# Decoder trunk on one core: the scores of gated linear attention on 32-column strips, the norm's sum of squares in two rounded matmuls

## The chip, the cores and the metric

One core of a Trainium2 chip. The metric is the device time of one execution in microseconds; the kernel before has a median of 2439.63 us over 3 runs (2439.05 to 2439.84). Engines are called as in the profile: PE is TensorE's matmul, PEld its weight load, DVE is VectorE, ACT ScalarE, POOL GpSimd, SP the engine that queues transfers.

## The reference, cut to what matters

Two layers, one even (retention and a gated recurrence), one odd (gated linear attention, GLA), each with a squared-ReLU MLP, for a prompt of 1024 tokens and eight samples of 8 tokens (64 tokens). Only the odd layer's mixer is touched:

```
def step(s, blk):                       # one chunk of one head, C = 64 or 8 in the reference
    qc, kc, vc, gc = blk
    b = jnp.cumsum(gc, axis=1)
    diff = b[:, :, None] - b[:, None, :]
    w = jnp.exp(jnp.where(causal[None, :, :, None, None], diff, -jnp.inf))
    scores = jnp.einsum('bihd,bjhd,bijhd->bhij', qc, kc, w)
    o = (jnp.einsum('bhij,bjhe->bihe', scores, vc)
         + jnp.einsum('bihd,bhde->bihe', qc * jnp.exp(b), s))
    ...
o = head_rms(o) * norm_w                # x * rsqrt(mean(x*x) + eps) over the 256 values of a head
mix = (jax.nn.silu(r) * o.reshape(B, T, GLA_VALUE)) @ w_out
```

## The kernel before

Everything is kept transposed: 128 features on the partitions, 1088 tokens (1024 + 64) along the free side, in three groups of 384, 384 and 320 tokens (`GROUPS`). A float32 product of the large projections is made of three matmuls on rounded parts (high x high, high x low, low x high, `mm`, line 732); GpSimd and ScalarE split the weights, VectorE empties PSUM.

In the odd layer a list written out in Python (`odd_schedule`, from line 232) sets one order for all engines: each engine walks it and does its share of each item, in that order, so no engine overtakes its own list. Four heads of nine chunks (`ORDER`: prompt chunks 0 to 5, then the 64 sample tokens, then 6 and 7). Projections of later units fill the gaps: an `S` item is one unit and group, cut into two halves where it stands between score items.

The scores of a chunk of 128 tokens are not made with one decay per pair. For seven levels v (0 to 6) the chunk is cut into blocks of 2 x 2^v tokens; keys in the left half and queries in the right half of a block are scaled relative to the block's middle (items `X`, `XE`, `Q`, made by VectorE and ScalarE per group of three chunks, signalled by `lev_ready`), and a product of the two gives the scores that cross that middle. The diagonal itself comes from plain k and q. TensorE does this in `score` (from line 1137) in two parts:

- item `A` (from line 1194): three transposes (lines 1211, 1213), then the plain product k x q over the full 128 x 128 (line 1220), then the coarse levels 6, 5, 4, where only the wanted blocks are computed: one 64 x 64, two 32 x 32, four 16 x 16 matmuls (line 1153);
- then one half projection of the list;
- item `A2`: the fine levels 3 to 0. Each is one matmul with all 128 key columns as weights and the 64 right-half query columns moving (line 1159); of its result only the entries in the level's blocks are used. The last matmul raises `gsc_done`.

VectorE then waits for `gsc_done` and copies with masks (lines 2495, 2499) into the score matrix for item `B`. The chunk of 64 sample tokens has the plain product of 64 x 64 in `A` and three fine levels in `A2`. The score matmuls are in float32, not rounded; each such matmul leaves two records in the trace.

```
 1153  last = nc.tensor.matmul(flat[left:left + width, right], both[:, left:left + width], both[:, right], ...)
 1159  last = nc.tensor.matmul(out, keys, halves(both, v)[1], start=True, stop=True)
```

Norm of a head: `GN1` squares on ScalarE and adds the two halves on VectorE (line 2541); `GNM` sums over partitions with a matmul of ones in float32 (line 1300), takes the logarithm on ScalarE; `GN2` scales. There are 11 such sums; the twelfth is made apart.

## Time and profile before

| | |
|---|---|
| median of 3 runs | 2439.63 us |
| the profiled execution | 2441.21 us |
| its span, first to last instruction | 2439.1 us |
| PE / DVE / ACT / POOL busy | 99 / 54 / 33 / 50 % |
| mean granted TensorE clock | 0.993 |
| the odd layer's mixer | about 1180 to 1600 us of the span |

A row of the timeline gives the start, the time from the first start to the last end, engine, line, operation and tiles; for a matmul, 128*64 is the size of the weights (partitions x columns) and 128x64 what moves through. Records of PE overlap: the next matmul starts long before the one ahead of it has left the array. So costs are taken from start to start.

### The profile page before, as it was taken

How to read it: one execution, taken by the hardware profiler on the slowest of the kernel's cores; microseconds unless marked ns; L12 is line 12 of the kernel's file. 1: busy time of each engine (PE TensorE's matmuls, PEld its weight loads, DVE VectorE, ACT ScalarE, POOL GpSimd, SP SyncE). 2: the span in 40 equal slices, each digit the busy share in tenths (PEclk: the TensorE clock that was granted, in tenths of full speed). 3: DMA queues.
4: the chain of work that ended last, by engine and by line, in shares of the span. 5: the costliest groups of instructions: out<-in, count | busy, mean ns of one | idle time of the engine just before them, and what ended most of it. 6: DMA issues, size and time to landing. Idle time of an engine off the chain costs nothing. (4 is left out here: it accounts for less than half of the span.)

```text
span 2439.1 us, 42031 instructions
## 1 busy us (share of the span) xinstructions
PE 2423.2 (99%) x16160; PEld 2380.3 (98%) x16160; DVE 1305.2 (54%) x2047; ACT 796.2 (33%) x1254; POOL 1211.9 (50%) x1445
## 2 busy tenths in 40 slices
PE   9999999999999999999999999999999999999998
PEld 9999999999999999999999999999999999999998
DVE  6763354345545545566666665554345545445566
ACT  4711442222222223223444564442222222222234
POOL 2454136465675666675201111146565665666681
PEclk9999999999999999999999999999999999999999
DMA  4123031111111111113111111131111111111112
GB/s 151 35 63 89 26 119 44 53 44 44 52 44 44 52 53 41 47 53 117 47 42 63 47 50 58 34 128 44 44 44 53 53 44 44 53 45 43 53 53 83
DMA packets 41023, 140.04 MB, mean 57 GB/s; under 512 B 6320, under 2 KB 10032, under 8 KB 39696
## 3 DMA queue, kind: packets, MB, share of 16 engines
q1 hardware_dynamic: 32768, 106.78, 13.8%
q10 hardware_dynamic: 8080, 30.78, 3.5%
q8 instruction: 128, 2.10, 0.4%
q14 instruction: 47, 0.39, 0.0%
HBM read 120.42 MB, written 14.88 MB: 55 GB/s over the span
## 5 line engine op out<-in xcount | busy, mean ns | idle before, releaser
L732 PE MATMUL PS<-RB,WH 128*128 128x384 f32 (+1 forms) x4368 | 1087.7, 330 | 0.0
L732 PEld LDWEIGHTS PS<-RB,WH 128*128 128x128 f32 x4368 | 773.5, 189 | 7.5 <-issue 3.6
L732 PE MATMUL PS<-RA,WH 128*128 128x272 f32 (+2 forms) x3520 | 769.0, 309 | 1.3 <-DVE RA L1868 0.7
L732 PE MATMUL PS<-RB,WL 128*128 128x384 f32 (+1 forms) x2232 | 731.6, 328 | 0.0
L638 POOL TENSOR_TENSOR WH<-WR,FEW 128x256 fp32r<-128x256 f32 x420 | 320.1, 792 | 622.3 <-PE PS L732 593.0
L732 PEld LDWEIGHTS PS<-RA,WH 128*128 128x128 f32 x3520 | 586.9, 188 | 5.8 <-DVE RA L1868 1.0
L732 PE MATMUL PS<-RA,WL 128*128 128x272 f32 (+2 forms) x1760 | 540.6, 307 | 0.0
L732 PEld LDWEIGHTS PS<-RB,WL 128*128 128x128 f32 x2232 | 421.4, 189 | 0.0
L642 POOL TENSOR_TENSOR WL<-WR,WH 128x256 fp32r<-128x256 f32 x420 | 372.8, 917 | 0.0
L732 PEld LDWEIGHTS PS<-RA,WL 128*128 128x128 f32 x1760 | 330.7, 188 | 0.0
L1967 DVE TENSOR_TENSOR X<-PS,X 128x544 f32<-128x544 f32 x280 | 202.6, 724 | 205.2 <-PE PS L732 205.1
L1908 DVE SCALAR_TENSOR_TENSOR RAW<-PS,RS 128x384 f32<-128x384 f32 (+1 forms) x192 | 97.0, 533 | 351.1 <-PE PS L732 317.9
L732 PE MATMUL PS<-RA,WS 128*128 128x272 f32 x2016 | 272.1, 288 | 0.0
L732 PEld LDWEIGHTS PS<-RA,WS 128*128 128x128 f32 x2016 | 260.5, 188 | 0.0
L661 POOL TENSOR_TENSOR WL<-WR,WH 128x512 fp32r<-128x512 f32 x168 | 155.2, 938 | 183.4 <-ACT WH L1400 183.4
L650 POOL TENSOR_TENSOR WL<-WR,WH 128x256 fp32r<-128x256 f32 x88 | 67.0, 792 | 336.5 <-ACT WH L1698 336.5
L1381 ACT ACTIVATE RAW<-RAW 128x384 f32<-128x384 f32 (+1 forms) x192 | 92.2, 505 | 332.2 <-DVE RAW L1908 332.2
L1919 DVE TENSOR_TENSOR RA<-RAW,RA 128x544 fp32r<-128x544 f32 (+1 forms) x112 | 142.9, 1294 | 26.3 <-ACT RA L1389 17.4
L661 POOL TENSOR_TENSOR WS<-WR,WS 128x256 fp32r<-128x256 f32 x112 | 119.1, 1064 | 14.6 <-ACT WS L1413 14.6
L1967 DVE TENSOR_TENSOR GA<-PS,GA 128x544 f32<-128x544 f32 x112 | 81.2, 725 | 80.0 <-PE PS L732 79.3
L1892 DVE TENSOR_TENSOR X<-PS,EB 128x384 f32<-128x384 f32 (+1 forms) x48 | 25.4, 535 | 116.6 <-PE PS L732 116.6
L1348 ACT ACTIVATE RB<-X,FEW 128x1088 fp32r<-128x1088 f32 x24 | 28.7, 1205 | 161.9 <-DVE X L1892 125.7
(237 smaller groups left out, 2370.8 us busy)
## 6 DMA issues: line engine op xcount, KB each, us to landing
WR<-ws SPq DMA_DIRECT2D x189, 512.0 KB, 3.5
EB<-xT ACTq DMA_DIRECT2D x8, 544.0 KB, 5.9
x_spill<-X ACTq DMA_DIRECT2D x8, 544.0 KB, 3.1
EB<-x_spill ACTq DMA_DIRECT2D x8, 544.0 KB, 6.8
GA<-st_gla ACTq DMA_DIRECT2D x4, 1024.0 KB, 4.8
glas_o<-GA ACTq DMA_DIRECT2D x4, 1024.0 KB, 4.6
yT<-X SPq DMA_DIRECT2D x16, 208.0 KB, 1.9
X<-xT ACTq DMA_DIRECT2D x4, 544.0 KB, 6.0
```

The lines of the kernel that those rows point to most:

```text
L638: nc.gpsimd.tensor_tensor(WH[:, slot, QC * q:QC * (q + 1)], WR[:, slot, QC * q:QC * (q + 1)], ZERO[:, 0:1].to_broadcast([P, QC]), ALU.add) ...
L642: nc.gpsimd.tensor_tensor(WL[:, slot, QC * q:QC * (q + 1)], WR[:, slot, QC * q:QC * (q + 1)], WH[:, slot, QC * q:QC * (q + 1)].bitcast(F32 ...
L650: nc.gpsimd.tensor_tensor(WL[:, slot, QC * q:QC * (q + 1)], WR[:, slot, QC * q:QC * (q + 1)], WH[:, slot, QC * q:QC * (q + 1)].bitcast(F32 ...
L661: return nc.gpsimd.tensor_tensor(out, of, high.bitcast(F32), ALU.subtract)
L732: return nc.tensor.matmul(out, lhsT, rhs, start=start, stop=stop, skip_group_check=True)
L1348: A(dst[:, 0, k, :], X[:, k, :], ACT.Copy, scale=scale).then_inc(h_high, counts)
L1381: A(RAW[:, j, grp(g)], RAW[:, j, grp(g)], ACT.Square).then_inc(sq_done, 1)
L1892: V.tensor_tensor(X[:, m, s:s + size], PS[:, bank(n0 + m, g), 0:size], EB[:, at(m), s:s + size], ALU.add).then_inc(psum_free, 2)
L1908: V.scalar_tensor_tensor(RAW[:, j, s:s + size], PS[:, 3 * (j % 2) + g, 0:size], 0.0, RS[:, s:s + size], ALU.max, ALU.mult).then_inc(psum_f ...
L1919: return V.tensor_tensor(BS[:, slots, 1, q, :], of, BS[:, slots, 0, q, :].bitcast(F32), ALU.subtract)
L1967: last = V.tensor_tensor(pair_of(to), PS[:, bank0:bank0 + 2, 0:BN], pair_of(to), ALU.add)
```

## The change

The array's 128 weight columns are addressed in strips of 32 (`BLOCK`); the 32 rows of a result that a strip makes lie on its own 32 partitions of PSUM. Of each product only the squares of 32 tokens are computed that hold wanted entries. A matmul with 32 weight columns and 16 or 32 moving ones replaces each quarter of a full one: four for the plain product (32 x 32), four for each fine level (32 x 16), two for level 6 (32 x 64). The split between `A` and `A2` stays at level 4, but the plain product of the 64-token chunk moves from `A` into `A2`. `gsc_done` rises by one for each strip at level 0, so the waits for it count strips (`scored`).

The norm's sum: VectorE writes the sum of the two squares as a rounded part and a rounded rest (two more operations, each waiting for the one ahead), and two rounded matmuls replace the float32 one. `ONES` becomes a rounded constant, written by an operation instead of a fill; other users read it as float32 (`ONE`).

```
-SPLIT = 4
+BLOCK = 32
...
+        ONES = sb("ONES", [P, P], F32R)
+        ONE = ONES[:, :].bitcast(F32)
...
+        gSQR = RAWR[:, :, :].rearrange("p k t -> p (k t)")[:, 1792:2560]
...
+        def scored(places):
+
+            return sum(CHUNKS[c][1] // BLOCK for _, c in PLACES[:places])
...
-                last = None
+                key, query = gK(h)[:, s:s + n], gQ(h)[:, s:s + n]
+                block = lambda b: slice(b, b + BLOCK)
+                for b in range(0, n, BLOCK) if c == LAST or levels[0] else ():
+                    nc.tensor.matmul(flat[block(b), block(b)], key[:, block(b)], query[:, block(b)], start=True, stop=True)
                 for v in reversed(levels):
...
+                    width = 1 << v
                     if v >= FINE:
...
-                            last = nc.tensor.matmul(flat[left:left + width, right], both[:, left:left + width], both[:, right],
-                                                    start=True, stop=True)
+                            for b in range(left, left + width, BLOCK):
+                                rows = slice(b, b + min(width, BLOCK))
+                                nc.tensor.matmul(flat[rows, right], both[:, rows], both[:, right], start=True, stop=True)
                         continue
-                    keys = both if v else gK(h)[:, s:s + n]
                     at = n + n // 2 * v
-                    out = flat[0:n, at:at + n // 2].rearrange("p (b n) -> p b n", n=1 << v)
-                    last = nc.tensor.matmul(out, keys, halves(both, v)[1], start=True, stop=True)
-                return last
+                    for b in range(0, n, BLOCK):
+                        out = flat[block(b), at + b // 2:at + (b + BLOCK) // 2].rearrange("p (b n) -> p b n", n=width)
+                        last = nc.tensor.matmul(out, (both if v else key)[:, block(b)], halves(both[:, block(b)], v)[1],
+                                                start=True, stop=True)
+                        if v == 0:
+
+                            last.then_inc(gsc_done, 1)
...
-                    nc.tensor.matmul(flat[0:n, 0:n], gK(h)[:, s:s + n], gQ(h)[:, s:s + n], start=True, stop=True)
-                    score(h, c, range(SPLIT, LEVELS) if c < LAST else ())
+                    if c < LAST:
+                        score(h, c, range(FINE, LEVELS))
...
-                    score(h, c, range(SPLIT) if c < LAST else range(SLEVELS)).then_inc(gsc_done, 1)
+                    score(h, c, range(FINE if c < LAST else SLEVELS))
...
-                        nc.tensor.matmul(PS[:, 7, 0:size], ONES[:, :], gSQ[:, 0:size], start=True, stop=True).then_inc(gn_ms, 1)
+                        mm(PS[:, 7, 0:size], ONES[:, :], gSQR[:, 384:384 + size], True, False)
+                        mm(PS[:, 7, 0:size], ONES[:, :], gSQR[:, 0:size], False, True).then_inc(gn_ms, 1)
...
-                    dve.wait_ge(gsc_done, k + 1)
+                    dve.wait_ge(gsc_done, scored(k + 1))
...
-                    V.tensor_tensor(gSQ[:, 0:size], gSQ[:, 0:size], gSQ[:, 384:384 + size], ALU.add).then_inc(gn_sum, 1)
+                    first, second = gSQ[:, 0:size], gSQ[:, 384:384 + size]
+                    link(V.tensor_tensor(first, first, second, ALU.add))
+                    link(V.tensor_scalar(gSQR[:, 384:384 + size], first, 0.0, None, ALU.add))
+                    V.tensor_tensor(gSQR[:, 0:size], first, gSQR[:, 384:384 + size].bitcast(F32), ALU.subtract).then_inc(gn_sum, 1)
```

What TensorE has in its list for the 64-token chunk of the first head, before (GA holds k, q and the levels, PS is PSUM; a row gives the partitions x columns of the result, so a result of 32 partitions is one strip):

```order
L1211 MATMUL PS<-CST,GA 64x128
L1213 MATMUL PS<-CST,GA 64x128 x2
L1220 MATMUL PS<-GA 64x64
L732 MATMUL PS<-RB,WH 128x320 x2
...
L732 MATMUL PS<-RB,WL 128x320
L1159 MATMUL PS<-GA 64x32 x3
L732 MATMUL PS<-RB,WH 128x320 x2
```

And with the change:

```order
L1224 MATMUL PS<-CST,GA 64x128
L1226 MATMUL PS<-CST,GA 64x128 x2
L738 MATMUL PS<-RB,WH 128x320 x2
...
L738 MATMUL PS<-RB,WL 128x320
L1152 MATMUL PS<-GA 32x32 x2
L1169 MATMUL PS<-GA 32x16 x6
L738 MATMUL PS<-RB,WH 128x320 x2
```

The plain product has gone from ahead of the half projection to behind it. The coarse part of the whole chunk that comes next, before:

```order
L1220 MATMUL PS<-GA 128x128
L1153 MATMUL PS<-GA 64x64
L1153 MATMUL PS<-GA 32x32 x2
L1153 MATMUL PS<-GA 16x16 x4
L732 MATMUL PS<-RB,WH 128x384 x2
```

And with the change:

```order
L1152 MATMUL PS<-GA 32x32 x4
L1164 MATMUL PS<-GA 32x64 x2
L1164 MATMUL PS<-GA 32x32 x2
L1164 MATMUL PS<-GA 16x16 x4
L738 MATMUL PS<-RB,WH 128x384 x2
```

Seven matmuls have become twelve in the same place; in `A2` four of 128x64 become sixteen of 32x16.

## Rows read from the trace of the kernel before

**Rows 1.** the page: span, and each engine's busy time

```profile
span 2439.1 us, 42031 instructions
...
PE 2423.2 (99%) x16160; PEld 2380.3 (98%) x16160; DVE 1305.2 (54%) x2047; ACT 796.2 (33%) x1254; POOL 1211.9 (50%) x1445
```

**Rows 2.** table by stage: length, busy time (instructions) of PE, PEld, DVE, ACT, POOL; clock; DMA

```profile
1180.00:1600.00 420.00, 418.37 (x3015) 397.47 (x3015) 260.43 (x688) 206.24 (x422) 72.01 (x96) 0.98 0.15 50
```

**Rows 3.** timeline of PE, coarse part of one whole chunk: start us, length us, what

```profile
1413.39 0.39 PE L1220 MATMUL PS<-GA 128*128 128x128 f32 x2
1413.71 0.56 PE L1153 MATMUL PS<-GA 128*64 128x64 f32 x14
1414.19 0.62 PE L732 MATMUL PS<-RB,WH 128*128 128x384 f32 x2
1414.65 0.34 PE L732 MATMUL PS<-RB,WL 128*128 128x384 f32 x1
```

**Rows 4.** the narrow records of that part: two windows of the timeline, and line L1153

```profile
1413.82 0.42 PE L1153 MATMUL PS<-GA 128*64 128x64 f32 x11
...
1413.97 0.30 PE L1153 MATMUL PS<-GA 128*32 128x32 f32 x12
...
L1153 PE MATMUL PS<-GA x14: 176/189/270, 1413.7 to 1414.1; 128*16 128x16 f32 x8, 128*32 128x32 f32 x4, 128*64 128x64 f32 x2
```

**Rows 5.** timeline of PE, fine part of the same chunk

```profile
1416.21 0.33 PE L732 MATMUL PS<-RB,WL 128*128 128x384 f32 x1
1416.38 1.00 PE L1159 MATMUL PS<-GA 128*128 128x64 f32 x8
1417.19 0.59 PE L732 MATMUL PS<-RB,WH 128*128 128x384 f32 x2
1417.62 0.33 PE L732 MATMUL PS<-RB,WL 128*128 128x384 f32 x1
```

**Rows 6.** timeline of PE, the 64-token chunk: A in one head, A2 in another

```profile
1440.40 0.38 PE L1213 MATMUL PS<-CST,GA 128*64 128x128 f32 x2
...
1441.42 0.34 PE L732 MATMUL PS<-RB,WL 128*128 128x384 f32 x1
...
1248.18 0.31 PE L732 MATMUL PS<-RB,WL 128*128 128x320 f32 x1
1248.42 0.54 PE L1159 MATMUL PS<-GA 128*64 128x32 f32 x6
1248.88 0.56 PE L732 MATMUL PS<-RB,WH 128*128 128x320 f32 x2
```

**Rows 7.** timeline of PE, a sum of squares

```profile
1431.85 0.81 PE L1300 MATMUL PS<-SMALL,ONES 128*128 128x384 f32 x2
1432.49 0.27 PE L1211 MATMUL PS<-CST,GA 128*128 128x128 f32 x1
```

**Rows 8.** a stretch at the lower clock: table by stage, and PE's timeline in it

```profile
1258.70:1265.40 6.70, 6.70 (x24) 5.85 (x24) 1.82 (x5) 0.00 (x0) 1.67 (x3) 0.50 0.20 78
...
1261.38 0.52 PE L732 MATMUL PS<-RB,WH 128*128 128x384 f32 x1
1261.70 0.52 PE L732 MATMUL PS<-RB,WL 128*128 128x384 f32 x1
```

**Rows 9.** timeline of DVE and PE: the addition of squares, and its sum

```profile
1233.45 0.56 DVE L2541 TENSOR_TENSOR SMALL<-SMALL 128x384 f32<-128x384 f32 x1 [1.32 <-ACT SMALL L1791]
...
1237.52 0.48 PE L1300 MATMUL PS<-SMALL,ONES 128*128 128x384 f32 x1
```

**Rows 10.** timeline of DVE and PE around the fine levels of a 64-token chunk

```profile
1432.14 0.49 DVE L1884 TENSOR_TENSOR GA<-PS,RS 128x320 f32<-128x320 f32 x1 [3.13 <-PE PS L732]
...
1439.27 0.56 DVE L1884 TENSOR_TENSOR SMALL<-PS,RS 128x384 f32<-128x384 f32 x1 [0.23 <-PE PS L732]
...
1443.88 0.54 PE L1159 MATMUL PS<-GA 128*64 128x32 f32 x4 [0.17 <-DVE GA L2479]
```

**Rows 11.** timeline of DVE behind the constants at the start

```profile
5.76 1.23 DVE L2104 TENSOR_TENSOR WL<-WR,WH 128x1024 fp32r<-128x1024 f32 x1 [3.66 <-ACT WH L1537]
```

More of the change, by code:

```diff
@@ L331, in build @@
         PRM, ZERO, EPST = FEW[:, 0:N_PRM], FEW[:, N_PRM:N_PRM + 2], FEW[:, N_PRM + 2:]
-        ONES = sb("ONES", [P, P])
+        ONES = sb("ONES", [P, P], F32R)
+        ONE = ONES[:, :].bitcast(F32)
         N_SMALL = 3456
@@ L794, in rms_group @@
                 s, size = GROUPS[g]
-                nc.tensor.matmul(PS[:, ms_bank(r, g), 0:size], ONES[:, :], RS[:, s:s + size],
+                nc.tensor.matmul(PS[:, ms_bank(r, g), 0:size], ONE, RS[:, s:s + size],
                                  start=True, stop=True).then_inc(ms_done, 1)
@@ L961, in last_rms @@
                 if g < 2:
-                    nc.tensor.matmul(PS[:, 7, 0:size], ONES[:, :], RS[:, s:s + size],
+                    nc.tensor.matmul(PS[:, 7, 0:size], ONE, RS[:, s:s + size],
                                      start=True, stop=True).then_inc(ms_done, 1)
                 else:
-                    nc.tensor.matmul(PS[:, 7, 0:size], ONES[:, :], RS[:, s:s + size], start=True, stop=False,
+                    nc.tensor.matmul(PS[:, 7, 0:size], ONE, RS[:, s:s + size], start=True, stop=False,
                                      skip_group_check=True)
                     pe.wait_ge(square_ready, 8 * 4 + KT * 3)
-                    nc.tensor.matmul(PS[:, 7, 0:size], ONES[:, :], last_square(KT - 1, size), start=False, stop=True,
+                    nc.tensor.matmul(PS[:, 7, 0:size], ONE, last_square(KT - 1, size), start=False, stop=True,
                                      skip_group_check=True).then_inc(ms_done, 1)
@@ L984, in head_sum @@
                     pe.wait_ge(s_updated, states_before(item))
-                nc.tensor.matmul(PS[:, norm_bank(g, h), 0:size], ONES[:, :], NB[:, h, 0:size],
+                nc.tensor.matmul(PS[:, norm_bank(g, h), 0:size], ONE, NB[:, h, 0:size],
                                  start=True, stop=True).then_inc(rn_ms, 1)
@@ L996, in _ @@
                         for _ in range(16):
-                            nc.tensor.matmul(PS[:, 7, 0:P], ONES[:, :], ONES[:, :], start=True, stop=True)
+                            nc.tensor.matmul(PS[:, 7, 0:P], ONE, ONE, start=True, stop=True)
                         first_step(0, RA0, 0)
@@ L1218, in _ @@
                         pe.wait_ge(gsc_masked, k - 1)
-                    flat = PS[:, score_bank(k), :]
-                    nc.tensor.matmul(flat[0:n, 0:n], gK(h)[:, s:s + n], gQ(h)[:, s:s + n], start=True, stop=True)
-                    score(h, c, range(SPLIT, LEVELS) if c < LAST else ())
+                    if c < LAST:
+                        score(h, c, range(FINE, LEVELS))
                 elif kind == "A2":
                     h, c = item[1:]
-                    score(h, c, range(SPLIT) if c < LAST else range(SLEVELS)).then_inc(gsc_done, 1)
+                    score(h, c, range(FINE if c < LAST else SLEVELS))
                 elif kind == "B":
@@ L1306, in last_head_sum @@
                 for v in range(2):
-                    last = nc.tensor.matmul(PS[:, 7, 0:320], ONES[:, :], gSQ[:, 384 * v:384 * v + 320], start=v == 0, stop=v == 1)
+                    last = nc.tensor.matmul(PS[:, 7, 0:320], ONE, gSQ[:, 384 * v:384 * v + 320], start=v == 0, stop=v == 1)
                 last.then_inc(gn_ms, 1)
@@ L1357, in rstd @@
                 other(ACT.Ln)
-                act.wait_ge(consts_set, 2)
+                act.wait_ge(consts_set, 3)
                 for g, (s, size) in enumerate(GROUPS):
@@ L1747, in _ @@
                         if e > 1:
-                            act.wait_ge(gsc_done, 3 * (e - 1))
+                            act.wait_ge(gsc_done, scored(3 * (e - 1)))
                         A(right, halves(gSP(h)[:, s:s + n], v)[1], ACT.Exp, scale=-1.0 / TAU).then_inc(x0_ready, 1)
@@ L1811, in _ @@
                     if k == 0:
-                        act.wait_ge(gsc_done, len(PLACES))
+                        act.wait_ge(gsc_done, scored(len(PLACES)))
                         act.wait_ge(gkv_turned, len(PLACES))
@@ L2090, in last_down @@
                 scale_out(2, KT - 1)
-            V.memset(ONES[:, :], 1.0).then_inc(consts_set, 1)
+            link(V.memset(EPST[:, 1:2], 1.0))
+            V.tensor_scalar(ONES[:, :], EPST[:, 1:2].to_broadcast([P, P]), 0.0, None, ALU.add).then_inc(consts_set, 2)
             V.memset(EPST[:, 0:1], EPS).then_inc(consts_set, 1)
-            V.memset(EPST[:, 1:2], 1.0).then_inc(consts_set, 1)
             V.memset(LW[:, :, :, :], 0.0).then_inc(lw_zero, 1)
@@ L2409, in _ @@
                         s, n = CHUNKS[c]
-                        keep = ONES[:, 0:n] if c < LAST else CST[:, G_RS:G_RS + TS]
+                        keep = ONE[:, 0:n] if c < LAST else CST[:, G_RS:G_RS + TS]
                         if c == LAST:
@@ L2445, in _ @@
                     if e > 1:
-                        dve.wait_ge(gsc_done, 3 * (e - 1))
+                        dve.wait_ge(gsc_done, scored(3 * (e - 1)))
                     w = gB(h)[:, s:s + n].rearrange("p (b n) -> p b n", n=2 << v)
```

1 line of the change is left out of this document (removed).

## The prediction

> **What bounds the kernel now.** I read the page first: TensorE is busy for 2423.2 of 2439.1 us, VectorE for about half [rows 1]. A busy matmul row is no proof of full use, so I went to the table of stages, cut at the odd layer's mixer (1180 to 1600 us), the only stretch that the change works in, apart from one constant at the start. There TensorE has 420.00 - 418.37 = 1.63 us without a matmul and VectorE 260 of 420 us of work [rows 2]. So TensorE sets the pace, and what a matmul costs is read from start to start, not from its duration, since each row overlaps the next. Then the timeline of TensorE, chunk by chunk. The pitch of 384 columns in the rounded type is (1416.38 - 1416.21) = 0.17 us; I use 0.174, the mean of many [rows 5]. A float32 matmul makes two records, and with 128 columns of weights one record takes (1417.19 - 1416.38)/8 = 0.10 us: the eight records of the fine levels move 64 columns each and would need half of that, so the weight load sets their pace [rows 5]. The places move in step: the same rows recur in all 32 whole chunks to within 0.02 us, but for one or two that wait for VectorE.
>
> **Coarse part of a whole chunk (A), before.** From where the first score record starts, 1413.39, to the third matmul behind the scores, 1414.65, it is 1.26 us; two of these matmuls cost 0.35 anyway, so the scores cost 0.91 [rows 3]. In it: the diagonal square and the way into narrow weights 1413.71 - 1413.39 = 0.32; the 64 x 64 block 0.11, and from its second record to the first of 32 columns 0.15; then twelve records of 32 and 16 columns. These twelve begin at 1413.97, and their common row ends 0.30 later with a record of 0.176, so the last starts at 1414.09: twelve starts in 0.12 us, **0.011 us a record** [rows 4]. They lie in different 32-column strips of the array, so the strips do work side by side. Then 0.10 to the first full matmul, whose successor is 0.28 instead of 0.17 behind it: leaving costs 0.10 + 0.11 = 0.21. Entering costs 0.32 - 2 x 0.11 = 0.09 to 0.10 [rows 3].
>
> **A after.** The diagonal becomes 4 matmuls (8 records) of 32 x 32, the 64 x 64 block 2 matmuls (4 records) of 32 weight columns x 64; the twelve stay. The fullest strip, the first, gets 2 + 2 + 2 records of those and 2 of the 16-wide. What a record costs inside one strip the trace bounds from both sides. Upper: weights and stream one after another; the 64 x 64 pair has 0.11 for 64 + 64 columns [rows 4], so 0.83 ns a column, and 32 + 32 give 0.053, 32 + 64 0.080. Lower: the load hides the stream; six records with 64 weight columns and 32 moving ones span 1248.74 - 1248.42 = 0.32 in five steps, 0.06 each [rows 6], so half as wide a load gives about 0.032. The strip then takes 0.43 or 0.28 us; I take the middle, 0.355, since both kinds occur in the rows nearest to it. A costs 0.09 + 0.36 + 0.21 = 0.66, **0.24 us less**.
>
> **Fine part (A2).** Before: from 1416.38 to 1417.62 less 0.35 is 0.89 us [rows 5]. After: 16 matmuls, 32 records of 32 weight columns x 16, eight in each strip. By the bounds a record costs 0.032 or 0.040 us in its strip, so 0.036 x 7 + 0.02 of stagger = 0.27 for the body; entry and exit, which this part did not have before, add 0.09 + 0.21. Sum 0.58, **0.31 us less**.
>
> **The 64-token chunk.** Its diagonal square leaves A for A2, so A loses a whole excursion: 1441.42 - 1440.51 - 0.11 - 0.35 = 0.45 us, 1440.51 (1440.40 + 0.38 - 0.27) being the last start of the transposes [rows 6]. A2 costs (1249.13 - 1248.33) - 0.15 = 0.65 before (the second matmul behind it starts at 1248.88 + 0.56 - 0.31; the one ahead of it was due to be followed at 1248.18 + 0.15), and after 0.09 + 0.35 (two 32 x 32 records and six of 32 x 16 in each of two strips) + 0.21 = 0.65. Four times 0.45 is **1.8 us**.
>
> **The norm sums.** One float32 matmul of ones takes 1432.49 - 1431.85 = 0.64 us for 384 columns [rows 7]; two rounded ones take 0.35. Eight such save 0.29 each, three of 320 columns (0.64 x 320/384 = 0.53 against 0.29) 0.24 each: **3.0 us**. VectorE gets two more operations per sum, each like the addition of 0.56 us [rows 9], with a wait for itself between: 1.2 us, or 11 x 1.2 = 13 us on an engine that is idle for 160. No TensorE step is queued behind it closely: the tightest sum is ready at 1234.01 and its matmul starts at 1237.52, 3.5 us later [rows 9]. Behind these operations on VectorE stand masks and copies, and within the same chunk it idles for 3.13 us [rows 10], so I cost them at nothing. If that cover were gone it would be 1.2 us at each of 11 places. The constant of ones is set in two steps instead of one, ahead of a stretch in which VectorE idles for 3.66 us [rows 11]: nothing. That the semaphore of the scores now rises by one per strip moves no other step.
>
> **What is given back.** TensorE is not alone everywhere. Inside the fine levels of the 64-token chunk it stands without work for 0.17 us until VectorE has made the second level. These levels end a chain on VectorE that runs without a gap from 1439.27 on, where it had waited 0.23 us for a projection [rows 10]. What TensorE gains behind that point is lost: this chunk's A part (0.45), and what of the gain of the chunk ahead (0.55) exceeds those 0.23. Together that is 0.77, of which I take 0.7 at each of four heads; plus 0.8 as an estimate, one such place more, for group starts elsewhere that leave VectorE no time: 0.7 x 4 + 0.8 = **3.6 us**. The first chunk of all, whose levels are made as TensorE asks for them, counts for nothing, hence 31 chunks below.
>
> **Sum.** 31 x (0.24 + 0.31) = 17.1; + 1.8 + 3.0 = 21.9; less 3.6 gives 18.3 us. The profiled execution took 2441.21 us, so 2422.9; the median of the runs, 2439.63, lies 1.6 us below that execution, and the same 18.3 us put the new median at **2421 us**.
>
> **Where a rule and a row disagree.** The rows show 0.011 us a record over four strips, and break-even lies where 54 record steps (23 + 31) and two ways in and out (0.61) equal today's 0.91 + 0.89 plus some 0.15 for the other gains per chunk: (1.95 - 0.61)/54 = 0.025 us a record. The Trainium skill, page "TensorE: Matmul & The Clock Gate", section "Wait — 56ns, not 53.3ns?", says that start-to-start never drops below about 25 ns however small a matmul is. By that rule the sum would be no gain at all. The trace disagrees, with 0.011 us for twelve records. The same page's section on the semaphore tail puts about 26 ns on each further increment at the end of a packed set; three more on 32 chunks would add 2.5 us if TensorE stood still for them, and no run here shows that yet.
>
> **Rivals.**
> - VectorE becomes the bound of the mixer. For it: TensorE already stands at such a place [rows 10], and VectorE has 13 us more to do. Against it: VectorE's 160 us of idle time [rows 2], and TensorE's 1.63 in the whole stage. If half of the gain were given back, 11 us remain: 2429.
> - A floor per start. If the instruction stream can feed only one narrow record per 0.025 us, a whole chunk costs 54 x 0.025 + 0.61 = 1.96 instead of 1.80, so +5.1; less 1.8 and 3.0: 2440. For it: twelve records are few, and could have been lined up during the drain ahead of them; 32 in a row may not be. Against it: nothing in rows 4 slows towards the end.
> - The strips do not overlap when neighbours in the order write the same bank in turn, so the quarters run one after another. This ends slower: A is 8 x 0.053 + 4 x 0.080 + 4 x 0.053 + 8 x 0.028 = 1.18, + 0.30 = 1.48 (+0.57); A2 is 32 x 0.040 + 0.30 = 1.58 (+0.69); 32 x 1.26 - 4.8 = +35.5: 2475. It decides from 0.025 us a record on. Against it stand the twelve records, which also write one bank.
> - The clock. In one stretch the granted clock is 0.50, the lower level of 1.2 GHz, and matmuls of 384 columns come 0.32 us apart instead of 0.17 [rows 8]. The stage's mean of 0.98 [rows 2] means that such stretches are 17 to 21 us in sum and cost some 9. Fewer or more of them shift the result by about 3 us either way; if the narrow scores of each of the 12 groups of chunks brought one half as long as that in rows 8, it would cost 12 x 3.35 x (1 - 0.17/0.32) = 19 us and leave nothing: 2440.
>
> **Chances.** The forecast 0.76; VectorE as the bound 0.12; the floor 0.06; the clock taking it all 0.03; serial strips 0.03. A measurement of this kernel tells 0.2%, 4.9 us, from no change. Faster: 0.76 + 0.12 = 0.88; within 0.2%: 0.06 + 0.03 = 0.09; slower 0.03. The range: the lower pitch throughout saves 32 x (0.08 + 0.03) = 3.5 more and the clock 3: 2415. The upper pitch costs as much, and VectorE's rival reaches to 2429; 2430 holds both.
>
> **What would show it.** In the changed trace A should cost about 0.66 and A2 0.58 by the same subtraction, with 32 records of A2 within 0.3 us; a sum of squares 0.35; TensorE's idle time before the fine levels of the 64-token chunks up by 2 to 4 us; the stage from 1180 on shorter by 18 us and everything else alike. It would be wrong if 32 narrow records took 0.8 us, or if the idle time ahead of group starts had grown by ten.

## The result and the profile after

The changed kernel takes **2413.56 us** (median of 4 runs, 2411.36 to 2414.48) against 2439.34 us (2437.56 to 2439.84, 4 runs) of the kernel before on the same chip: ratio 0.9893, 95% interval [0.9881, 0.9905], so 25.8 us faster. The forecast was 2421.0 with a range of 2415 to 2430. The direction was right, and so was the main mechanism; the gain is 7.5 us larger than the 18.3 forecast, and the result lies 1.4 us below the range. The profiled execution took 2414.09 us, 27.1 below that of before. The page answers to [rows 1], the stage table to [rows 2]:

```profile
span 2412.0 us, 44170 instructions
...
PE 2394.8 (99%) x17216; PEld 2348.2 (97%) x17216; DVE 1315.7 (55%) x2069; ACT 796.0 (33%) x1254; POOL 1221.5 (51%) x1445
```

```profile
1180.00:1600.00 420.00, 416.93 (x4230) 391.55 (x4228) 285.28 (x731) 217.50 (x437) 89.89 (x112) 0.98 0.19 63
```

TensorE is still the bound, at 99%, with 1056 more matmul records in less time. VectorE has 10.5 us more work over the whole span (13 were expected). In the fixed stretch of 420 us TensorE's time without a matmul rose from 1.63 to 3.07 us: small beside the gain.

Where the time went is read off one mark, the first transpose of the last chunk. Before, and then after:

```profile
1587.84 0.27 PE L1211 MATMUL PS<-CST,GA 128*128 128x128 f32 x1
```

```profile
1560.91 0.51 PE L738 MATMUL PS<-RAWR,ONES 128*128 128x384 f32 x2
1561.26 0.27 PE L1224 MATMUL PS<-CST,GA 128*128 128x128 f32 x1
```

It comes 1587.84 - 1561.26 = 26.6 us earlier, so nearly the whole 27.1 us was gained in the mixer. The first of these two rows of after is the norm sum: two rounded matmuls, 1561.26 - 1560.91 = 0.35 us where the float32 one took 0.64 [rows 7].

The coarse part of a whole chunk, TensorE's timeline of after (it answers to [rows 3]):

```profile
1399.14 0.38 PE L1226 MATMUL PS<-CST,GA 128*128 128x128 f32 x2
1399.46 0.27 PE L1152 MATMUL PS<-GA 128*32 128x32 f32 x8
1399.54 0.38 PE L1164 MATMUL PS<-GA 128*32 128x64 f32 x16
1399.85 0.61 PE L738 MATMUL PS<-RB,WH 128*128 128x384 f32 x2
1400.30 0.34 PE L738 MATMUL PS<-RB,WL 128*128 128x384 f32 x1
```

The last transpose starts at 1399.14 + 0.38 - 0.27 = 1399.25; one of these holds the array for 0.11, so the scores' turn begins at 1399.36. To the third matmul behind them it is 0.94, less 0.35: **0.59 us** (forecast 0.66, before 0.91). The first score record comes 0.21 behind the transpose instead of 0.11: the way in costs 0.10. The 24 records then start between 1399.46 and about 1399.75 (the row ends at 1399.92, its last record being 0.175 long): 0.29 us, where I had chosen 0.355 between 0.28 and 0.43. The way out is 0.10 + 0.11 (1400.30 - 1399.85 = 0.45 holds two matmuls that cost 0.35 elsewhere), as before.

The fine part (for [rows 5]), the timeline, and the same records as one tile of one line (duration min/median/max in ns, first and last start):

```profile
1401.88 0.34 PE L738 MATMUL PS<-RB,WL 128*128 128x384 f32 x1
1402.15 0.44 PE L1169 MATMUL PS<-GA 128*32 128x16 f32 x32
...
1402.98 0.34 PE L738 MATMUL PS<-RB,WL 128*128 128x384 f32 x1
...
L1169 PE MATMUL PS<-GA x32: 182/183/204, 1402.2 to 1402.4; 128*32 128x16 f32 x32
```

1402.98 - (1401.88 + 0.174) - 0.35 = **0.58 us** (forecast 0.58, before 0.89). All 32 records start within 0.44 - 0.18 = 0.26 us: 0.0084 us a record over four strips, 0.034 within one.

The 64-token chunk where nothing waits (fourth head; for [rows 6]):

```profile
1531.04 0.38 PE L1226 MATMUL PS<-CST,GA 128*64 128x128 f32 x2
...
1531.62 0.34 PE L738 MATMUL PS<-RB,WL 128*128 128x384 f32 x1
...
1533.18 0.34 PE L738 MATMUL PS<-RB,WL 128*128 128x384 f32 x1
...
1534.26 0.34 PE L738 MATMUL PS<-RB,WL 128*128 128x384 f32 x1
```

`A`: from the last transpose (1531.15) to the third matmul 0.47 us, where it was 0.91: 0.44 less (forecast 0.45). `A2`: 1534.26 - 1533.18 - 0.174 - 0.35 = 0.56, where I had 0.65 both before and after.

What TensorE waits for, in the mixer, before and after (us, times, longest):

```profile
PE PS L1159 <- DVE GA L2479: 1.3, 2, 1.1
```

```profile
PE PS L1169 <- DVE GA L2492: 2.4, 6, 0.8
PE PS L1164 <- DVE GA L2492: 0.6, 1, 0.6
```

With 0.2 us behind another level before, 1.5 us became 3.0. The forecast was that 3.6 us would be given back here. The longest of before, 1.1 us, is gone and others stand elsewhere, the longest in the third head:

```profile
1427.67 0.24 PE L1169 MATMUL PS<-GA 128*32 128x16 f32 x4 [0.81 <-DVE GA L2492]
```

The table counts only the time in which the profile has TensorE idle. From start to start the stretching is larger: over what the same records need undisturbed, 2.5 us before (0.20, 0.47 and 1.45 at the 64-token chunk of heads two to four, 0.37 at another chunk) and 3.5 us after (1.17 and 1.58 in heads two and three, 0.78 at another chunk). So 1.0 us was given back by starts, 1.5 by the table. Experiments 9, 10 and 12 are about who causes these waits.

**The clock** differs a little between the two profiled executions. In the mixer, this is the table by stage over the places with a granted clock below 1 (length, busy times, then PEclk behind POOL), before and after (before also a fourth, 1580 to 1588, with 0.79 as the second):

```profile
1256.00:1268.00 12.00, 12.00 (x64) 11.02 (x63) 5.99 (x16) 3.62 (x10) 2.77 (x4) 0.72 0.12 45
1355.00:1363.00 8.00, 8.00 (x45) 7.28 (x45) 6.74 (x16) 5.96 (x11) 3.12 (x4) 0.79 0.05 9
1454.00:1472.00 18.00, 18.00 (x100) 16.72 (x100) 8.95 (x22) 7.77 (x13) 3.13 (x4) 0.81 0.10 30
```

```profile
1250.00:1262.00 12.00, 12.00 (x101) 10.91 (x99) 8.51 (x23) 5.78 (x17) 2.83 (x4) 0.86 0.17 45
1345.00:1351.00 6.00, 6.00 (x31) 5.58 (x31) 5.86 (x14) 4.17 (x7) 2.08 (x3) 0.72 0.00 0
1438.00:1450.00 12.00, 12.00 (x66) 11.13 (x67) 9.31 (x20) 6.37 (x13) 3.75 (x4) 0.72 0.15 45
```

At the lower level (a clock of 0.50) for 2 x (0.28 x 12 + 0.21 x 8 + 0.19 x 18 + 0.21 x 8) = 20 us before and 2 x (0.14 x 12 + 0.28 x 6 + 0.28 x 12) = 13 us after. By the price of [rows 8], 1 - 0.17/0.32, those 7 us are worth 3.2 of the 26.6. Runs of one kernel differ in the same way: the changed kernel took 2417.65 and 2417.70 at a mean clock of 0.993, 2414.09 and 2414.48 at 0.994, and 2410.79 to 2413.03 at 0.996. So a share of the gap in the profiled pair is the clock and not the change: some 23.4 us are the change's own. Two other readings agree. The profiled run of experiment 6 is the changed kernel with some 20 us at the lower level in the mixer, as many as before: 2441.21 - 2417.65 = 23.6 us. And a straight line of time against mean clock through all recorded runs (42 of the kernel before, 12 of the changed one) gives 2438.5 and 2414.3 us at 0.9945, 24.2 us apart, with about 2 us for each 0.001 of clock. The mean clock is recorded to 0.001 only, so a comparison "at equal clock" below is good to 1 or 2 us.

### The profile page after: what moved, and what is told of

Read it like the earlier page. It is cut to its first block and busy times, and to the rows that moved or that the text cites. A ratio compares the mean times of both kernels' runs of the same rounds, so it can differ in the third digit from the quotient of the medians.

```text
span 2412.0 us, 44170 instructions
## 1 busy us (share of the span) xinstructions
PE 2394.8 (99%) x17216; PEld 2348.2 (97%) x17216; DVE 1315.7 (55%) x2069; ACT 796.0 (33%) x1254; POOL 1221.5 (51%) x1445
## 5 line engine op out<-in xcount | busy, mean ns | idle before, releaser
L648 POOL TENSOR_TENSOR WL<-WR,WH 128x256 fp32r<-128x256 f32 x420 | 374.7, 922 | 0.0
L656 POOL TENSOR_TENSOR WL<-WR,WH 128x256 fp32r<-128x256 f32 x88 | 70.1, 827 | 313.2 <-ACT WH L1711 313.2
L1905 DVE TENSOR_TENSOR X<-PS,EB 128x384 f32<-128x384 f32 (+1 forms) x48 | 25.4, 535 | 116.2 <-PE PS L738 116.2
```

The source lines that it names most:

```text
L648: nc.gpsimd.tensor_tensor(WL[:, slot, QC * q:QC * (q + 1)], WR[:, slot, QC * q:QC * (q + 1)], WH[:, slot, QC * q:QC * (q + 1)].bitcast(F32 ...
L656: nc.gpsimd.tensor_tensor(WL[:, slot, QC * q:QC * (q + 1)], WR[:, slot, QC * q:QC * (q + 1)], WH[:, slot, QC * q:QC * (q + 1)].bitcast(F32 ...
L1905: V.tensor_tensor(X[:, m, s:s + size], PS[:, bank(n0 + m, g), 0:size], EB[:, at(m), s:s + size], ALU.add).then_inc(psum_free, 2)
```

## Experiments

Each ratio is to the kernel before, on the same chip; the experiments ran on four chips, and the median of the kernel before was 2439.18 to 2439.58 us on each, so they are compared with the changed kernel across chips too. Three theories stood at the start: strips work side by side with the load of 32 columns as the pitch; a floor per start; and a clock or VectorE share in the gain.

**1. The norm sums alone** (scores as before).

```
+  mm(PS[:, 7, 0:size], ONES[:, :], gSQR[:, 384:384 + size], True, False)
+  mm(PS[:, 7, 0:size], ONES[:, :], gSQR[:, 0:size], False, True).then_inc(gn_ms, 1)
   score(h, c, ...)      # unchanged from before
```

> The change's norm sums alone, scores as before. Theory A (each part saves what its own matmuls on TensorE lose, and the parts add): 8 x 0.29 + 3 x 0.25 = 3.1 us, so about 2436 us, with the sum of squares at 0.35 us and no new idle time. Rival B (the surplus over my forecast comes from the norm, which frees more than its own time): 6 us or more, 2433 or less. Rival C (the surplus is the clock: other stretches at the lower clock than before): the saving differs from 3.1 by 1.5 or 3 us, in the same direction as the length of the stretches at the lower clock.

2435.01 us (2430.59 to 2437.23, 10 runs), ratio 0.9982 [0.9972, 0.9992]: 4.2 us less than before (2439.18). The 3.0 of the sum lies within the interval (2.0 to 6.8 us). The seven runs at a clock of 0.994 have a mean of 2436.2, against 2439.6 for the kernel before at that clock: 3.5 us. TensorE's waits in the mixer are 0.7 us here, where they were 1.5: with new work on VectorE they are shorter, not longer, which no theory had expected, and which fits what experiments 9 to 12 say of these waits.

**2. The strips alone** (the norm sum in float32 again).

```
-  mm(... gSQR ...) x2; two more VectorE operations
+  nc.tensor.matmul(PS[:, 7, 0:size], ONE, gSQ[:, 0:size], start=True, stop=True).then_inc(gn_ms, 1)
```

> The scores on strips alone, norm sums as before. Theory A: 31 x (0.32 + 0.32) + 4 x 0.55 = 22 us on TensorE, less some 1 to 2 us more of waiting for VectorE, so 2418 to 2420 us plus or minus the clock. Rival B: 2420 or more. Rival C: the profile has about 7 us less at the lower clock than before, and without that the saving is 19 us or less.

2417.95 us (2416.50 to 2419.33), ratio 0.9910 [0.9893, 0.9926]: 21.2 us less. With experiment 1 that adds up to 25.4, against 25.8 for both together, so the parts add up within what these runs tell, and VectorE's extra work at the norm costs TensorE nothing that shows. TensorE's waits are 3.5 us here, 0.7 in experiment 1 and 3.0 with both: they do not add up one by one.

**3. Strips in the coarse part only** (fine levels full width, norm as before).

```
-  for b in range(0, n, BLOCK): ... 32x16 per strip
+  out = flat[0:n, at:at + n // 2].rearrange("p (b n) -> p b n", n=width)
+  last = nc.tensor.matmul(out, both if v else key, halves(both, v)[1], start=True, stop=True)
```

> Strips in the coarse part (and for the plain product of the 64-token chunk, which is in A2), the fine levels on full weights as before, norm sums as before. Theory A: 32 x 0.32 = 10 us in A and about 1 us at the 64-token chunks, so about 2428 us, and A2 costs 0.89 us as before. My forecast's middle pitch would have given 32 x 0.24 = 8 us, 2431. Rival C: the deviation from 2428 goes with the stretches at the lower clock.

2426.43 us (2425.51 to 2428.21), ratio 0.9947 [0.9930, 0.9963]: 12.8 us less. The fine part costs what it did:

```profile
1407.05 1.00 PE L1168 MATMUL PS<-GA 128*128 128x64 f32 x8
```

By the rows of after, the coarse part gives 31 x 0.32 = 9.9 and the 64-token chunk's moved product 4 x 0.44 = 1.8, together 11.7. Had the coarse part given only the forecast 0.24, it would be 9.2. At an equal clock the runs say 11.4 (2428.21 against 2439.6 at 0.994, 2426.1 against 2437.5 at 0.995); the rest of the 12.8 is the clock. The remaining 21.2 - 12.8 = 8.4 us are the fine part (31 x 0.31 = 9.6 by the forecast).

**4. Same matmuls, other neighbours:** the fine part strip by strip instead of level by level.

```
-  for v in reversed(levels): for b in range(0, n, BLOCK): ...
+  for b in range(0, n, BLOCK): for v in reversed(levels): ...
```

> The changed kernel, but the fine part goes through the strips in the outer loop and the levels in the inner one, so eight records in a row fall to one strip. If strips overlap only while neighbours in the order lie in different strips, the body of A2 goes from 0.26 us to 32 x 0.03 = 1.0 us and the kernel gets slower by 32 x 0.7 = 23 us: about 2436. If TensorE takes records out of a long window past a busy strip, as the order of the records in the coarse part hints, nothing changes: 2414. In between, with a short window: 2418 to 2430.

2431.69 us (2425.14 to 2434.04), ratio 0.9957 [0.9940, 0.9974]: 18 us slower than the changed kernel, with the same work. Two of its four runs had a clock of 0.992, lower than any run of the changed kernel; at 0.994 it is 15 us (2429.39 against 2414.3), at 0.996 13.5 (2425.14 against 2411.7). The 32 records:

```profile
1413.74 0.89 PE L1161 MATMUL PS<-GA 128*32 128x16 f32 x32
```

They span 0.89 - 0.18 = 0.71 us instead of 0.26: 0.023 us a record, and 32 x 0.45 = 14.4 us for the kernel, as the runs at equal clock say. Strips overlap only for instructions that are close together in the list: eight records of one strip stand in line, and the next strip's first one starts at 1413.894, when five of those eight have started. It is neither the full serial sum (31 x 0.034 = 1.05) nor free. The order of the list alone decides over more than half of the gain.

**5. The levels of the 64-token chunk in another order** (2, 1, 0 ahead of levels 4 and 3 of the same group, so that they are made earlier).

```
+    if e % 3 == 2:
+        return x(1) + [("XE", e, 0)] + q(2, 1), q(0, 4, 3)
```

> The changed kernel, but VectorE makes the levels that the 64-token chunk needs (2, 1, 0) ahead of levels 4 and 3 of its group, which only the next chunk needs. If TensorE's idle time ahead of that chunk (in the profile 1.2 us in the second head, 1.6 in the third) is the end of the VectorE chain, it shrinks by the two products of level 4 and 3, 0.8 us, in each, and nothing new is late, since levels 4 and 3 had over 6 us to spare: 1.6 us less. If it is set by something ahead of these products (ScalarE's table or the projection), it stays.

2414.36 us (2412.41 to 2418.15), ratio 0.9898 [0.9882, 0.9915]: no gain. TensorE's waits:

```profile
PE PS L1171 <- DVE GA L2490: 1.2, 3, 0.4
...
PE PS L740 <- ACT X L1794: 1.0, 3, 0.4
```

With two more of 1.2 and 0.6 us behind other levels that makes 4.0 us instead of 3.0: more and shorter waits, now also for level 0 and for ScalarE. From start to start the second and third head's chunks lose 0.92 and 0.95 us instead of 1.17 and 1.58, so the end of VectorE's chain had some part in it, but another order only shifts the waits.

**6 and 11. The changed kernel again**, beside the others.

> The changed kernel once more, beside the others, to measure the scatter of its runs with the granted clock: 2411 to 2415 us, the faster ones with the higher mean clock.

> The changed kernel once more beside these two, as their base and for the scatter with the clock: 2411 to 2418 us.

Experiment 6, then 11: 2414.64 us (2411.32 to 2417.70), ratio 0.9893 [0.9877, 0.9910], and 2411.47 us (2410.79 to 2412.34, all at a clock of 0.996), ratio 0.9887 [0.9872, 0.9902]. The result holds; a difference under some 3 us between two variants is not read as one unless their clocks agree.

**7. Every fine matmul issued twice** (64 records instead of 32 per whole chunk).

```
+  if c < LAST:
+      nc.tensor.matmul(out, (both if v else key)[:, block(b)], halves(both[:, block(b)], v)[1], start=True, stop=True)
```

> The changed kernel with each fine matmul of a whole chunk issued twice, 64 records instead of 32 (same result). Theory A (a record costs its strip 0.032 us, four strips side by side, however many): the body of A2 goes from 0.26 to 0.52 us, + 32 x 0.26 = 8 us, about 2422. A floor per start behind a queue that was filled ahead: the second half comes at 0.025 us a record, + 0.8 us a chunk, 2439.

2426.53 us (2422.91 to 2427.50), ratio 0.9941 [0.9925, 0.9958]: 12 to 13 us above the changed kernel (some 11 at an equal clock), 0.65 - 0.26 = 0.39 us per chunk by the rows: the two lines' records as tiles, and the first and last of them in the timeline.

```profile
L1170 PE MATMUL PS<-GA x32: 182/183/203, 1408.9 to 1409.5; 128*32 128x16 f32 x32
L1172 PE MATMUL PS<-GA x32: 182/183/183, 1409.0 to 1409.5; 128*32 128x16 f32 x32
...
1408.88 0.26 PE L1170 MATMUL PS<-GA 128*32 128x16 f32 x7
1408.96 0.18 PE L1172 MATMUL PS<-GA 128*32 128x16 f32 x1
...
1409.49 0.22 PE L1172 MATMUL PS<-GA 128*32 128x16 f32 x3
```

64 records start in 1409.49 + 0.22 - 0.18 - 1408.88 = 0.65 us: 0.010 us each. A floor of 0.025 would need 1.6. Twice the records make 2.5 times the body. Each pair now lies in one strip, so this may be experiment 4's effect in small; nothing else was tried for it.

**8. Wider strips** (`BLOCK` 64 instead of 32: half the matmuls, twice the columns).

```
-BLOCK = 32
+BLOCK = 64
```

> The changed kernel with BLOCK = 64: two strips of 64 instead of four of 32. With a record's cost in its strip set by the weight load (0.058 us for 64 columns in the trace of before), the body of A2 is 8 x 0.058 = 0.46 us instead of 0.26; in A the plain product takes two records of 64 x 64 in each strip and level 6 is one 64 x 64 matmul as before, then the way from strips of 64 to strips of 32 costs 0.15 again: some 0.15 us more. Together 32 x 0.35 = 11 us slower than the changed kernel, 2425. If the number of records or of starts counted, 64-wide blocks with half the matmuls would be no slower.

2427.51 us (2425.88 to 2429.44), ratio 0.9951 [0.9934, 0.9967]: about 13 us slower than strips of 32 (14 at an equal clock).

```profile
1409.86 0.66 PE L1169 MATMUL PS<-GA 128*64 128x32 f32 x16
...
1406.97 0.34 PE L1152 MATMUL PS<-GA 128*64 128x64 f32 x4
1407.13 0.28 PE L1164 MATMUL PS<-GA 128*64 128x64 f32 x2
```

Fine part: 16 records start in 0.66 - 0.22 = 0.44 us; eight lie in each half, so seven steps of 0.06 in a half, against 0.034 with 32 weight columns and 0.10 with 128 [rows 5]. The two lower rows are the start of the coarse part, 64 x 64 throughout. The last record of line 1152 starts at 1407.31 - 0.22 = 1407.09, some 0.11 behind the first of its half; the next in that half come at 1407.13 and 1407.19. So the first step behind the switch into narrow weights is 0.11, and from then on it is 0.05 to 0.06 with 64 moving columns, as it is with 32. In the changed kernel the same holds for 32 weight columns: 0.03 a step with 16 or 32 moving columns, 0.06 with 64. In all of these the pitch goes with whichever is wider, the weights or what moves; the other hides.

**9, 10 and 12. Who makes VectorE late at the 64-token chunk.** The trace of before, VectorE and GpSimd ahead of the longest wait (fourth head), and TensorE's wait:

```profile
1554.17 3.05 POOL L650 TENSOR_TENSOR WL<-WR,WH 128x256 fp32r<-128x256 f32 x4 [16.44 <-ACT WH L1698]
...
1554.21 0.88 DVE L2478 TENSOR_TENSOR GA<-GA 128x160 f32<-128x160 f32 x1
...
1557.46 0.54 PE L1159 MATMUL PS<-GA 128*64 128x32 f32 x4 [1.14 <-DVE GA L2479]
```

The level products, 0.32 us by themselves, take 0.84 to 0.88 while GpSimd splits a weight piece. In the changed kernel the split falls behind the chain in the fourth head and further onto it in the second (and third):

```profile
1329.23 3.09 POOL L656 TENSOR_TENSOR WL<-WR,WH 128x256 fp32r<-128x256 f32 x4 [18.14 <-ACT WH L1711]
...
1329.90 0.55 DVE L1897 TENSOR_TENSOR SMALL<-PS,RS 128x384 f32<-128x384 f32 x1
...
1330.91 0.82 DVE L2491 TENSOR_TENSOR GA<-GA 128x128 f32<-128x128 f32 x1
...
1332.40 0.28 DVE L2491 TENSOR_TENSOR GA<-GA 128x128 f32<-128x128 f32 x1
...
1333.80 0.24 PE L1169 MATMUL PS<-GA 128*32 128x16 f32 x4 [0.40 <-DVE GA L2492]
...
1532.11 0.32 DVE L2491 TENSOR_TENSOR GA<-GA 128x160 f32<-128x160 f32 x1
...
1533.02 3.65 POOL L656 TENSOR_TENSOR WL<-WR,WH 128x256 fp32r<-128x256 f32 x4 [15.78 <-ACT WH L1711]
```

Three kernels hold the split of such a piece back on ScalarE, which starts it. Experiment 10 does so in the kernel before, fourth head alone; 9 in the changed kernel, heads two to four, until the levels are ready; 12 likewise, but until after the copy of chunk 5's result.

```
+HELD = {1: 104, 2: 109, 3: 115}      # experiment 10: {3: 115}
-                    next_high(B_ODD_IN + item[1] + 1)
+                    if B_ODD_IN + item[1] + 1 not in HELD.values():
+                        next_high(B_ODD_IN + item[1] + 1)
+                if kind == "A2" and item[2] == LAST and item[1] in HELD:    # 9 and 10
+                    act.wait_ge(lev_ready, nth("Q", 3 * item[1] + 2, 0))
+                    next_high(HELD[item[1]])
+                    if c == 5 and h in HELD:                                # 12, behind the copy
+                        act.wait_ge(lev_ready, nth("Q", 3 * h + 2, 0))
+                        next_high(HELD[h])
```

> The kernel before, with the same hold in the fourth head alone. There TensorE stood 1.4 us ahead of the fine levels, while four VectorE products took 0.84 to 0.88 us each beside GpSimd (1554.2 to 1557.2). If GpSimd's work is the cause, they take 0.32 each, 2.2 us earlier in sum, the idle time goes from 1.4 to nothing, and the kernel is 1.4 us faster, plus or minus the clock. If not, it stays at 1.4.

2437.88 us (2431.54 to 2439.81, 11 runs), ratio 0.9993 [0.9984, 1.0002]. One gap of 1.4 us (by starts; 1.14 in the table) is at the edge of what the runs tell (about 1.5 us less than before at an equal clock), but the trace is plain:

```profile
1552.66 0.32 DVE L2483 TENSOR_TENSOR GA<-GA 128x160 f32<-128x160 f32 x1
...
1555.13 3.25 POOL L651 TENSOR_TENSOR WL<-WR,WH 128x256 fp32r<-128x256 f32 x4 [18.95 <-ACT WH L1699]
```

With GpSimd out of the way all products take 0.32, and TensorE's wait there is gone. So VectorE's length of chain was not what made it late there, its neighbour was. The hold also moves ScalarE's part of the split, but ScalarE is not the neighbour in question: in the third head of the kernel before, the products take 0.31 to 0.32 us (1442.80 to 1443.74) while ScalarE works almost without a break (1442.71 to 1444.43) and GpSimd has nothing to do.

> The changed kernel, but in the second, third and fourth head ScalarE rounds the next unit's weights (and so GpSimd makes their rest) only after the levels of the 64-token chunk are ready, instead of at the half projection ahead. In the changed trace VectorE's products take 0.82 to 0.83 us instead of 0.28, and a 0.48 us subtraction 1.02, while GpSimd works on these weights (1329.2 to 1332.3, 1422.7 to 1426.0). If that is what makes TensorE wait ahead of the 64-token chunk, its idle time there shrinks by 1.2 us in the second head and about 1.3 in the third, and stays near nothing in the fourth: about 2.4 us less in all, 2412. If the overlap is a coincidence and the products wait for their input, the idle time stays, or grows since ScalarE now stands in a wait.

2418.99 us (2416.22 to 2423.37), ratio 0.9923 [0.9910, 0.9937]: some 5 us slower than the changed kernel, 4.5 at an equal clock of 0.994. A miss. TensorE's waits, then GpSimd and VectorE one chunk later:

```profile
PE PS L739 <- ACT X L1797: 2.9, 2, 1.5
PE PS L1170 <- DVE GA L2497: 1.2, 4, 0.5
```

```profile
1432.50 3.35 POOL L657 TENSOR_TENSOR WL<-WR,WH 128x256 fp32r<-128x256 f32 x4 [25.33 <-ACT WH L1712]
...
1433.67 2.47 DVE L2431 TENSOR_TENSOR_SCAN X<-ONES,X 128x128 f32<-128x128 f32 x3
```

The waits for the fine levels fell from 2.4 to 1.2 us, but the split now lies on the scans (2.47 us for three, where three such scans take 1.06 in the changed kernel), ScalarE does its part just ahead of the copy (line 1797), and TensorE waits 1.5 us for that. The waits for the levels by starts are 0.53 and 0.55 us in heads two and three, from 1.17 and 1.58: shorter by 0.6 and 1.0, where 1.2 and 1.3 were expected. With 0.6 us more for a coarse level the waits are 4.7 us instead of 3.0, 1.7 more. Of the rest of the 4.5, 1.8 us lie ahead of the mixer, which the hold does not touch: the first transpose starts at 1203.33 us instead of 1201.53, with a wait of TensorE of 2.2 us that the changed kernel's third profile (experiment 11) has too. So the hold itself costs less than the 4.5 us.

> The changed kernel with the split of three weight pieces (heads 1, 2 and 3, the ones that GpSimd and ScalarE work on beside the level chain of the 64-token chunk) held back until behind ScalarE's copy of chunk 5's result, not merely until the levels are ready. Theory (GpSimd's work slows VectorE's products from 0.3 to 0.8 us, and in the run that held it until the levels were ready ScalarE's share of the split, about 1 us, only came later in front of the copy): TensorE's gaps ahead of the coarse and fine levels of the 64-token chunk in heads 1 and 2 shrink by 0.6 and 1.0 us as there, its waits for ScalarE's copy of 1.5 us each are gone, and the time is 1 to 2 us below the changed kernel, about 2412. Rival (any later place only moves the collision, now onto the scans of the next group or the weights' due time): waits of 1 us or more for ScalarE, POOL or the weights in each of the three heads, 2415 to 2419.

2413.91 us (2411.09 to 2416.44), ratio 0.9904 [0.9888, 0.9921].

```profile
PE PS L1170 <- DVE GA L2497: 1.2, 4, 0.5
PE PS L1165 <- DVE GA L2497: 0.5, 1, 0.5
PE PS L739 <- DVE RA L2597: 0.3, 1, 0.3
```

2.0 us of waits instead of 3.0, and those for the copy are gone as expected; the time is that of the changed kernel. The profiled execution is 3 us lower, at a clock of 0.995 against 0.994, which accounts for most of it; at 0.994 its three runs have a mean of 2414.7, the changed kernel's two 2414.3. A gain of the 1 us that the waits give would be below what these runs tell. No version tried is measurably faster than the changed kernel.

## Why the prediction was right in part, and where it failed

The result lies outside the range because two terms of the sum were mis-sized, both in the same direction: what the coarse part saves (0.24 us a chunk forecast, 0.32 measured, 2.5 us in all) and what is given back to VectorE (3.6 us forecast, 1.0 to 1.5 measured). Some 2 us of clock came on top.

**The bound, and the method.** TensorE was and is the bound, and start-to-start costs from single chunks carry over to the whole: the gain lies in the mixer, 26.6 of 27.1 us.

**The coarse part: the term that was mis-sized.** "I take the middle, 0.355": the rows gave 0.29, the lower of my two bounds, so `A` saves 0.32 and not 0.24, 31 x 0.08 = 2.5 us. The upper bound rested on the 0.11 us of the 64 x 64 pair [rows 4], read as weights and stream one after another. Experiment 8 shows what it was: the first step behind the switch into narrow weights, which happens once; the steps behind it, 64 x 64 alike, take 0.05 to 0.06. So the one row of the upper bound was part of the way in, and the six records in 0.32 us [rows 6] were the ones to go by.

**The fine part.** 0.58 forecast, 0.58 measured, with body (0.27 against 0.26) and both passages as put down. The body is partly luck: the middle pitch of 0.036 does not occur. In the first strip the first step is 0.052 and the other six 0.031 to 0.032, the lower bound; the mean of the seven is 0.034. A whole chunk saves 0.32 + 0.31 to 0.32 = 0.64: 31 x 0.64 = 19.7 instead of 17.1 us.

**The 64-token chunk.** 0.44 in `A` as forecast, and 0.1 more in `A2` its body again at the lower pitch: 2.2 instead of 1.8 us.

**The norm sums.** 0.64 to 0.35 as forecast, 3.1 us by rows; the runs of experiment 1 say 4.2 with an interval that holds it. VectorE's two operations cost nothing that shows (experiments 1 and 2 add up).

**What is given back: the other step that failed.** "0.7 x 4 + 0.8 = 3.6": I priced the wait by what TensorE gains behind the point where VectorE last waits for it, the same at four heads, from one head's rows. Measured is 1.5 us by the table of waits and 1.0 by starts. The 0.8 for "one such place more" came true (0.78, a coarse part in the first head). The 0.7 at each of four heads did not: by starts it is nothing in the first head, 0.97 and 1.11 in the second and third, and 1.45 less than before in the fourth.

GpSimd explains where these waits stand, but not why they are smaller than forecast. That it lengthens VectorE's chain is shown by experiment 10 for the kernel before, and by the fall of the waits in 9 and 12 for the changed one. Its share is about the same in both: before 1.8 us (1.45 in the fourth head and the 0.37 at another chunk there, where products of 128x192 take 0.90 instead of 0.35 us beside it), after 1.7 (3.5 less the 1.8 that experiment 12 leaves). The change moved it from one head to others, and it drops out of the difference. What is left without it is 0.20 and 0.47 before and 0.55 and 0.55 in experiment 12 for heads two and three, so 0.35 and 0.08 given back there instead of 0.7 each, nothing in the first and fourth, and 0.74 at the one place more. Why most heads have that much slack was not traced.

**The sum by measured terms.** 19.7 + 2.2 + 3.1 - 1.5 = 23.5 us (24.0 with 1.0 given back), against 23.4 at the mark once the clock's 3.2 is taken off, and 24.2 from the line through all runs. The forecast's 18.3 misses it by 2.6 (scores), 0.4, 0.1 and 2.1 (given back); the rest of the 7.5 us, some 2, is the clock. That the first chunk was left out of the 31 is within the rounding: what it saves it waits for VectorE.

**The clock** was forecast neutral within 3 us; that is what it does, in the profiled pair 3 us in the change's favour. It had no part in the gain beyond that: the stretches are of the same kind, at about the same places, 13 us instead of 20, and the 12 groups of narrow scores brought none. Their sum changes from execution to execution: the changed kernel's other two profiled runs have some 20 and 10 us of them in the mixer.

**The rivals.** A floor per start: refuted, 0.0084 us a record in the changed kernel and 0.010 with 64 in a row (experiment 7). The Trainium skill, page "TensorE: Matmul & The Clock Gate", section "Wait — 56ns, not 53.3ns?", has the start-to-start pace of about 25 ns as a floor; with matmuls of different column strips side by side the trace does not show it. The Trainium skill, page "TensorE: Matmul & The Clock Gate", section "Measured speedup vs the span model", puts packed tiles about 4 ns apart; that is the nearer rule here, though in the trace the first records of the four strips start 6 to 7 ns apart, and the mean of all 32 is 8.4. The semaphore's four increments at the end of the fine part cost no 2.5 us either: from the last start (1402.41) to the next full matmul it is 0.12 us, 0.10 in the coarse part, which raises none. Serial strips: refuted for this order, though experiment 4 shows how it would look, some 14 us for the same matmuls in another order. My condition for it was "neighbours that write the same bank in turn"; what decides is whether neighbours lie in the same strip. VectorE as the bound: refuted, the waits stay at 3 us (3.5 by starts).

**The range.** It ended at 2415 because lower pitch and clock were counted once each from 2421; with the lower pitch throughout (3.5), the clock (3), and the waits not given back (3.6) it would have reached 2411, and each of the three came in part. That the waits could be smaller than estimated was no bound of the range, and should have been.

## What to carry to other kernels

Small float32 matmuls are paced by the wider of their weights and what moves, most often the weights. Cut to strips of 32 columns they run four abreast, if neighbours in the list lie in different strips, for some 0.3 us on the way in and out (0.58 less 0.26 in the fine part). Before pricing a wait for another engine, read it at every place where it recurs, and look at who works beside that engine: one operation here has two durations, and a change that only shifts the timing moves it from one to the other. And compare at equal granted clock where a few us matter.

## What the runs showed that I had not expected

- GpSimd beside VectorE: a product of 128 x 160 float32 takes 0.85 instead of 0.32 us, three scans 2.47 instead of 1.06, for as long as GpSimd's subtractions of 128 x 256 run (3.0 to 3.7 us for four). ScalarE's part of the same split holds up a copy that stands behind it in ScalarE's list (experiment 9).
- It depends on where VectorE reads: the operation of line 1897, with one input in PSUM, takes its usual 0.55 us in the middle of GpSimd's work, while the products, whose two inputs both lie in SBUF, take 0.82. The Trainium skill, page "GPSIMD Engine Reference", section "Specifications", says the same: the two engines share their SBUF interfaces, and VectorE's operations with two SBUF inputs contend. The trace agrees, and gives it a size. Two inputs are not needed in every case: the norm's new rounding (line 2556, one input, in SBUF) takes 0.66 instead of 0.36 us at the one sum, 1543.62, where GpSimd works beside it.
- Records of different strips do not keep the order of the list. In experiment 7 each matmul of line 1170 (two records) is followed by its twin of line 1172, yet seven records of line 1170 start before the first of 1172: later strips start ahead of a twin that has to queue in its own.
- Strips look ahead only a little: eight records of one strip in a row keep most of the others idle for most of their time (0.71 us for 32 records, 0.26 with strips alternating), and with pairs in one strip the pace is 0.010 instead of 0.0084 us a record.
- The pitch inside a strip goes with the wider of weights and moving columns: 0.03 us for 32, 0.06 for 64 of either; with 128 weight columns it is 0.10 [rows 5].
